# HGRN2 heads of a hybrid decoder step: transposes of keys and values ahead of the scores on TensorE

## The reference

```python
b = jnp.cumsum(log_f, axis=1)
decay = jnp.where(causal, jnp.exp(b[:, :, None] - b[:, None, :]), 0.0)
scores = jnp.einsum('bthk,btshk,bshk->bhts', q, decay, k)
o = jnp.einsum('bhts,bshv->bthv', scores, v) + jnp.einsum('bthk,bhkv->bthv', q * jnp.exp(b), s0)
s_new = jnp.exp(b_last)[..., None] * s0 + jnp.einsum('bshk,bshv->bhkv', k * jnp.exp(b_last[:, None] - b), v)
```

## Time and profile before

| | |
|---|---|
| median of 3 runs | 1731.16 us (1731.08 to 1731.27) |
| profiled execution, its time | 1731.35 us |
| its span | 1729.8 us |
| PE busy | 1517.0 us, 88% of the span |
| DVE busy | 958.0 us, 55% |
| ACT busy | 672.3 us, 39% |
| POOL busy | 124.0 us, 7% |
| mean granted PE clock | 0.938 |

### The profile page before, as it was taken

How to read it: one execution, slowest core, us unless ns; L and a number is a source line. 1 busy time by engine, 2 the same in 40 slices (tenths; PEclk the granted TensorE clock), 3 DMA queues, 4 the chain that set the end, 5 groups by cost and what they waited for, 6 DMA issues and landing times.

```text
span 1729.8 us, 31847 instructions
## 1 busy us (share of the span) xinstructions
PE 1517.0 (88%) x12113; PEld 1227.6 (71%) x12113; DVE 958.0 (55%) x1677; ACT 672.3 (39%) x960; POOL 124.0 (7%) x110
## 2 busy tenths in 40 slices
PE   4588899878699999999866998988787999999994
PEld 3477777766578888788745777776665888887883
DVE  4766665555665555533375767565467555553334
ACT  3645533333354334422155554333326344432213
POOL 2100010000200000000030000000002000000002
PEclk8788999998899999999978989999898999999997
DMA  6122242221123332233321222233131322323321
GB/s 174 41 56 70 74 114 75 84 75 52 61 74 97 97 97 80 68 91 98 83 67 49 75 74 75 65 87 91 46 98 49 97 87 83 97 82 85 88 67 52
DMA packets 175037, 137.24 MB, mean 79 GB/s; under 512 B 5064, under 2 KB 169192, under 8 KB 174776
## 3 DMA queue, kind: packets, MB, share of 16 engines
q1 hardware_dynamic: 168192, 113.46, 22.5%
q0 software_dynamic: 5408, 18.60, 4.0%
q10 hardware_dynamic: 1372, 4.32, 0.8%
HBM read 124.28 MB, written 12.07 MB: 79 GB/s over the span
## 4 chain that ended last, share of the span: by engine, by line
PE 68%; DVE 13%; ACT 7%; DVEq 5%; issue 5%; ACTq 1%; DMA 1%; SPq 0%
PE ACC L508 58%; DVEq L1272 2%; PE SCR L538 2%; DVE X L1202 1%; PE OT L596 1%; DVE Z L1233 1%; DVE VX L1317 1%; ACT WH L839 1%; DVE WL L1162 1%; PE SCR L659 1%; DVE shared L1378 1%; DVE T L1271 1%; PE OT L595 1%; DVE B L1221 1%; DMA shared<-in_x_prompt_dram 1%
## 5 line engine op out<-in xcount | busy, mean ns | idle before, releaser
L508 PE MATMUL ACC<-XH,WH 128*128 128x280 f16 x2432 | 498.9, 287 | 74.9 <-DVE XL L1205 44.0
L508 PE MATMUL ACC<-XL,WH 128*128 128x280 f16 x2432 | 498.3, 287 | 0.0
L508 PE MATMUL ACC<-XH,WL 128*128 128x280 f16 x2432 | 497.7, 287 | 0.0
L508 PEld LDWEIGHTS ACC<-XH,WH 128*128 128x128 f16 x2432 | 238.0, 103 | 132.5 <-DVE XL L1205 46.5
L1162 DVE SCALAR_TENSOR_TENSOR WL<-stage,WH 128x2048 f16<-128x2048 f32 (+1 forms) x116 | 245.9, 2120 | 133.3 <-ACT WH L839 120.2
L508 PEld LDWEIGHTS ACC<-XL,WH 128*128 128x128 f16 x2432 | 241.4, 99 | 57.0
L508 PEld LDWEIGHTS ACC<-XH,WL 128*128 128x128 f16 x2432 | 241.7, 99 | 56.4
L839 ACT ACTIVATE WH<-stage 128x2048 f16<-128x2048 f32 (+1 forms) x116 | 204.8, 1765 | 102.0 <-PE ACC L508 86.8
L508 PE MATMUL ACC<-shared,WH 128*128 128x280 f16 x1408 | 225.3, 283 | 0.4 <-issue 0.3
L508 PEld LDWEIGHTS ACC<-shared,WH 128*128 128x128 f16 x1408 | 137.6, 98 | 31.0 <-issue 0.9
L508 PE MATMUL ACC<-shared,WL 128*128 128x280 f16 x704 | 141.4, 283 | 0.0
(11 more groups left out here) (258 smaller groups left out, 1802.7 us busy)
## 6 DMA issues: line engine op xcount, KB each, us to landing
stage<-in_w_in_dram SPq DMA_DIRECT2D x64, 512.0 KB, 5.3
stage<-in_w_a_dram SPq DMA_DIRECT2D x44, 512.0 KB, 4.4
stage<-in_w_b_dram SPq DMA_DIRECT2D x44, 512.0 KB, 4.6
stage<-in_w_down_dram SPq DMA_DIRECT2D x32, 384.0 KB, 3.3
stage<-in_w_down_dram SPq DMA_DIRECT2D x32, 320.0 KB, 3.7
out_dram<-shared POOLq DMA_DIRECT2D x16, 512.0 KB, 3.9
stage<-in_w_o_dram SPq DMA_DIRECT2D x16, 512.0 KB, 4.5
shared<-in_state_hgrn_dram POOLq DMA_DIRECT2D x8, 512.0 KB, 5.9
```

The source lines that it names most:

```text
L508: last = mm(ACC[:, acc, h, 0:HALF], lhs, x[:, xk + k, h * HALF:(h + 1) * HALF], start=begin, stop=end)
```

## The change

The four transposes move from slots 7 to 10 to slots 1 to 4, and the seven score jobs from slots 1 to 7 to slots 4 to 10. In slot 4 the last transposes are issued ahead of the first scores. ACT and DVE step through the PSUM jobs in the new order; the order of their own instructions stays as it is.

```diff
-                steps = [(slots[0][n], lambda n=n: scores(n)) for n in range(len(HG_JOBS))]
-                steps += [(slots[1][n], lambda n=n: transposes(n)) for n in range(4)]
+                steps = [(slots[1][n], lambda n=n: transposes(n)) for n in range(4)]
+                steps += [(slots[0][n], lambda n=n: scores(n)) for n in range(len(HG_JOBS))]
...
 # ACT
             def hg_stages(l, p):
                 s = scr_hg(l, p)
-                for b, _, _ in HG_JOBS:
-                    s.job(b)
 
                 def d():
+                    for b, _, _ in HG_JOBS:
+                        s.job(b)
                     for b in (1, 0, 1, 0):
                         s.job(b)
                     hg_d(l, p, s)
...
 # DVE
             def hg_stages(l, p):
                 s = scr_hg(l, p)
 
+                for b in (1, 0, 1, 0):
+                    s.job(b)
+
                 def states():
-                    for b in (1, 0, 1, 0):
-                        s.job(b)
                     low_sample(l * 2 * HEADS + p, HG_K_SCALE)
                     hg_states(l, p, s)
...
-HG_SLOTS = ([1, 2, 3, 4, 5, 6, 7], [7, 8, 9, 10], [12, 13], [22, 22], [23, 23, 24, 24, 25, 25], [28, 28], [14, 15, 16, 17, 18, 19, 20, 21])
+HG_SLOTS = ([4, 5, 6, 7, 8, 9, 10], [1, 2, 3, 4], [12, 13], [22, 22], [23, 23, 24, 24, 25, 25], [28, 28], [14, 15, 16, 17, 18, 19, 20, 21])
-HG_SLOTS_RT = ([1, 2, 3, 4, 5, 6, 7], [7, 8, 9, 10], [12, 13], [15, 16], [18, 19, 20, 21, 22, 23], [27, 27], [7, 8, 9, 10, 11, 12, 13, 14])
+HG_SLOTS_RT = ([4, 5, 6, 7, 8, 9, 10], [1, 2, 3, 4], [12, 13], [15, 16], [18, 19, 20, 21, 22, 23], [27, 27], [7, 8, 9, 10, 11, 12, 13, 14])
```

## The result

The changed kernel takes 1807.74 us (median of 4 runs, 1805.99 to 1809.12), the kernel before 1731.22 beside it: 1.0437 times as long, interval 1.0418 to 1.0455. The change costs 76.5 us where 57.7 were forecast. The profiled execution took 1809.12 us with a span of 1807.5.

A forecast was written before the change was run, and what follows sets the result against it. HGRN2 groups were taken as bound by a loop through PE, ACT and DVE. Terms of 34 + 4.6 + 19.1 = 57.7 us on 1731.35 gave 1789.05, 1789.0 for the median; 8-in-10 range 1766 to 1809.

The forecast's parts named there:

- The new wait: PE at transposes 2 (L571), second and third groups: idle 4.1 us until ACT has read transposes 0 (L919).
- Who ends last: Start of ACT's gate (L883): DVE's L1211 takes over after 1.8 us of slack, making L883 8.5 us later.
- The first groups: First HGRN2 group of each layer: scores 4.1 us later, cost 2.3 us each, 4.6 together, 4 to 8.
- How long the clock stays low: Clock at 0.50 when PE resumes after the new wait: 5 us assumed, losing 0.9 us after the first scores start.
- Behind L621 in the retention group: Longer idle stretch, some 4.4 us, makes the clock fall newly in layer 0: 1.7 us added, 0 to 5.
- second groups: Second HGRN2 group of each layer, forecast like the third: 8.5 us later; four such groups 34 us, 24.8 to 44.4.
- retention groups to L621: Retention group: last scores 10.3 us later, key rotation and L621 8.7 later, 6.4 to 11.2.
- The clock stays low for long: Rival: clock low for 10.1 us after each resume, so 1804 us; chance 0.15.
- The clock does not fall: Rival: the clock does not fall in the new wait, or falls late: 1773 us; chance 0.15.
- Without a new wait: Rival: only later scores, each of eight groups costs about 2.3 us: 18 us, 1749; chance 0.08.
- No change: Rival: the gain and the cost meet within the slack; chance 0.02.
- faster: Rival: ACT's reads still end last, L883 up to 1.8 us earlier in six groups: 14 us less, 1717; chance 0.03.

## Why the prediction was right, and where its size was off

*The new wait* was forecast at 4.1 us at L571, released by ACT's L919, and none in the first group. It is 3.84, 3.82 and 3.50 in layer 0, by L919, and none in the first group. `scores(0)` waits 0.46 us, forecast 0.4.

*Who ends last.* Forecast: DVE's gate read takes over from ACT, after 1.8 us of slack, and L621 waits about 6 us. L883 begins when DVE's L1211 has ended, and L621 waits 5.99. From the mean square to L883 the third group has 28.09 us for 20.13, which is 7.96 later (forecast 8.5), the second 10.58. The experiment with the gate's read moved shows the slack before; the one with the split moved shows DVE as the condition after.

*The first groups*: 2.48 and 3.00, forecast 2.3.

*How long the clock stays low* is the step that failed in its size: "I take 5, nearest to the 4.25 us row, where products and scores follow the resume as here." Measured are 9.1, 3.2 and 9.2 us. With these the prediction's own arithmetic gives 10.5 (half of 153.70 - 147.98 is lost, and not 0.9), 7.6 and 10.7, where the second group's way to L883 grew by 10.58, the third's by 7.96, and the retention group's way to L621 by 10.85. So the formula held, and its input was off, to either side.

*Behind L621 in the retention group* is the larger miss: "in layer 0 it is new, and I add 1.7 us (half of 3.4), from 0 to 5." The wait there is 4.25 us, forecast 4.4, but the clock was low for 9.5 us and for 3.3 more after the wait of 1.52. The way from L621 to L659 grew from 22.65 to 28.86 in layer 0 and from 24.33 to 28.87 in layer 1: 6.2 and 4.5, 10.7 together for 1.7. In layer 1 I had counted nothing, "the 0.50 is there already"; but the row of 2.10 us that I read shows a part of it only. It was some 3.4 us long and became as long as in layer 0:

```profile
1083.20:1086.50 3.30, 3.30 (x15) 2.01 (x14) 2.43 (x4) 1.91 (x1) 1.02 (x2) 0.50 0.06 20
```

In the third group of layer 0 the low stretch behind L621 went from 6.8 to 7.0 us, and nothing was the right count; in the second it went from 8.1 to 10.1, the last 1.0 of its 11.59.

The terms, forecast and measured: first groups 4.6 and 5.5; second groups 17.0 and 22.1; third groups 17.0 and 15.4; retention groups to L621 17.4 and 21.7; from L621 1.7 and 10.7; outside the groups 0 and 2.3. That is 57.7 and 77.7. The 2.3 are no part of the change as far as can be seen: the first group begins at 85.45 us before, at 86.55 in the changed kernel, and at 85.31 when it was run again, where the stages sum to 74.7 of the 75.5 us between the spans.

That the time still lies in the range, 1.3 us below its end, is in part luck. The term behind L621 measured 10.7 where its bounds were 0 and 5; the sum stayed inside because the first and third groups came out some 9 us below their upper bounds (5.5 for 8, 15.4 for 22.2).

*The rivals.* "The clock stays low for long", 1804, came closest in time, yet not as it was told: it is low for long in two of three places. "The clock does not fall" is refuted by the windows; the run with PE kept busy shows what it would have given, 1787.6 with the added products' own price. Without a new wait the order costs 22 us, as the run with ACT's reads first showed. "No change" is refuted by the result. For "faster" DVE's read of the gate tile would have to come no later than before; with that and two more moves arranged, the kernel with the new order does gain 0.4%.

*What stays open*: why the same wait before the same work is followed by 9.1 us of low clock in one group, 3.2 in the next, and 3.3 in both when DVE's order differs. The runs show that the lengths repeat from one execution to the next, and that they were others in the run whose stages ahead had other lengths; they do not show the rule.

## What to carry to other kernels

A job that is moved ahead on one engine is worth what its last consumer's other conditions leave: list for each start the conditions on all engines and their slack (here 1.8 us on DVE), and move their order along, or the gain becomes a wait. Price a new wait of some 4 us on TensorE as the wait and the low clock behind it, and behind each wait that it makes longer; for the length of a low stretch reckon with both ends, some 3 and 10 us here, and not with the middle. The best versions found leave the scores first and pull ACT's gate between its reads: 1714 to 1716 us, about 1% under the kernel before.

## What the runs showed of the hardware

DVE and POOL held each other up where two operations met. POOL's 1.91 us operation beside a clamp made that 2.00 us for 0.45, beside a tensor-tensor operation 2.14 for 0.66, and beside the product L1310 (128x560, 0.74 by itself) 2.46. It was itself held up, 2.27 and 2.78, when DVE's operation had begun first. Not every pairing did this: in the run with POOL a little later, a product that reads PSUM (L1281) took its 0.74 us beside POOL's 1.91. The Trainium skill, page "SBUF — State Buffer", section "SBUF: two separate sides", says that the two share one pair of ports, which whichever begins first holds until its instruction ends; in these pairings the traces agree. For DVE it names operations with two inputs in SBUF (L1281 has one, its other input lies in PSUM) and a faster mode; the clamp reads one tile, and no run here shows its mode by itself.

The clock's low stretches can be shortened by adding work: 30 unused products (3.74 us) in a wait took 20 us off the kernel. And a wait of 1.5 to 1.8 us kept the clock in some kernels and lost it in others, behind the same instruction; in the kernel before, the retention group's wait at L621 kept it in layer 0 (1.81 us) and lost it in layer 1 (1.80 us).
